# Second feed-forward projection of a hybrid decoder: seven block products for two of three token chunks

## The reference, cut to what matters

```python
x = _layer_norm(DN_ALPHA * x + mix, p['ln_mix_g'][i], p['ln_mix_b'][i])
hid = jnp.square(jax.nn.relu(x @ p['ffn_w1'][i]))                 # 1024 -> 4096
x = _layer_norm(DN_ALPHA * x + hid @ p['ffn_w2'][i], ...)          # 4096 -> 1024
```

## Time and profile before

| | us |
|---|---|
| median of 3 runs | 3169.58 (3167.16 to 3170.78) |
| profiled execution, its own time | 3167.34 |
| its span, first to last instruction | 3165.6 |
| PE busy | 3055.3 (97%) |
| weight loads (PEld) busy | 2841.0 (90%) |
| DVE busy | 1586.9 (50%) |
| POOL busy | 830.0 (26%) |
| ACT busy | 790.2 (25%) |

### The profile page before, as it was taken

One profiled execution on the slowest core, in us unless ns is written; L12 is line 12 of the kernel. 1 busy time (PEld: TensorE's weight loads), 2 busy tenths in 40 slices (PEclk: granted clock), 3 DMA queues, 4 the chain that ended last, 5 costly groups with the idle time before them and its releaser, 6 DMA issues.

```text
span 3165.6 us, 50120 instructions
## 1 busy us (share of the span) xinstructions
PE 3055.3 (97%) x20024; PEld 2841.0 (90%) x20024; DVE 1586.9 (50%) x2318; ACT 790.2 (25%) x1475; POOL 830.0 (26%) x523
## 2 busy tenths in 40 slices
PE   7998899999999999999989999998999999999997
PEld 7885789999999998999967878777999999999996
DVE  4877454333333354443358687878227333333335
ACT  4000442011111124111144444534106111111113
POOL 2232113333323232333201110113414232333330
PEclk9999999999999999999989999999999999999999
DMA  7555311111111113323255564747311111111111
GB/s 217 148 133 138 94 33 54 47 46 46 46 40 50 43 41 119 119 101 114 85 181 205 203 237 179 251 162 278 102 35 54 41 53 40 53 46 46 46 34 55
DMA packets 277968, 317.92 MB, mean 100 GB/s; under 512 B 25877, under 2 KB 217621, under 8 KB 276610
## 3 DMA queue, kind: packets, MB, share of 16 engines
q1 hardware_dynamic: 257577, 250.01, 25.6%
q10 hardware_dynamic: 12960, 40.04, 3.3%
q0 software_dynamic: 7296, 25.96, 2.4%
HBM read 224.63 MB, written 92.19 MB: 100 GB/s over the span
## 4 chain that ended last, share of the span: by engine, by line
PE 79%; DVE 10%; ACT 6%; issue 4%; DMA 1%; SPq 0%; POOL 0%; another core or an unknown queue 0%; DVEq 0%; ACTq 0%; POOLq 0%
PE ps L403 23%; PE ps L404 22%; PE ps L405 22%; PE ps L2068 2%; PE ps L1128 2%; PE ps L1171 1%; DVE CB L2489 1%; ACT X L486 1%; DVE CT L1565 1%; PE ps L1137 1%; PE ps L1138 1%; DVE RST L1729 1%; PE ps L1139 1%; PE ps L424 1%; DVE HT L1747 1%
## 5 line engine op out<-in xcount | busy, mean ns | idle before, releaser
L403 PE MATMUL ps<-AH,WH 128*128 128x352 f32 x3072 | 1000.4, 326 | 6.2 <-ACT SO L849 4.1
L404 PE MATMUL ps<-AL,WH 128*128 128x352 f32 x3072 | 986.2, 321 | 0.0
L405 PE MATMUL ps<-AH,WL 128*128 128x352 f32 x3072 | 985.7, 321 | 0.0
L388 POOL TENSOR_SCALAR WH<-RAW 128x1024 fp32r<-128x1024 f32 x200 | 236.0, 1180 | 1663.5 <-PEq L410 1467.7
L403 PEld LDWEIGHTS ps<-AH,WH 128*128 128x128 f32 x3072 | 577.6, 188 | 31.5 <-issue 22.6
L404 PEld LDWEIGHTS ps<-AL,WH 128*128 128x128 f32 x3072 | 578.7, 188 | 1.1 <-issue 0.2
L405 PEld LDWEIGHTS ps<-AH,WL 128*128 128x128 f32 x3072 | 577.5, 188 | 0.0
L390 POOL TENSOR_TENSOR WL<-RAW,WH 128x1024 fp32r<-128x1024 f32 x200 | 517.3, 2587 | 16.7
L403 PE MATMUL ps<-HH,WH 128*128 128x352 f32 x1536 | 498.4, 324 | 0.0
L404 PE MATMUL ps<-HL,WH 128*128 128x352 f32 x1536 | 492.2, 320 | 0.0
L405 PE MATMUL ps<-HH,WL 128*128 128x352 f32 x1536 | 491.9, 320 | 0.0
(11 more groups left out here) (317 smaller groups left out, 3392.3 us busy)
## 6 DMA issues: line engine op xcount, KB each, us to landing
RAW<-in_ffn_w SPq DMA_DIRECT2D x128, 512.0 KB, 3.6
CT<-in_state_mlstm_C SPq DMA_DIRECT2D x32, 1024.0 KB, 5.5
out_C_s<-CT SPq DMA_DIRECT2D x32, 1024.0 KB, 5.4
RAW<-in_ml_w_in SPq DMA_DIRECT2D x32, 512.0 KB, 3.9
RAW<-in_conv_w_pw SPq DMA_DIRECT2D x24, 512.0 KB, 7.9
STK<-u_scratch SPq DMA_DIRECT2D x64, 184.0 KB, 3.8
xc_scratch<-XC ACTq DMA_DIRECT2D x16, 528.0 KB, 2.7
so_scratch<-SO ACTq DMA_DIRECT2D x16, 528.0 KB, 3.7
```

Source lines behind the costliest of these rows:

```text
L388: pool.tensor_scalar(WH[:, k % 4], RAW[:, k % 2], 1.0, 0.0, ALU.mult, ALU.add).then_inc(w_hi, 1)
L403: pe.matmul(ps[:, bank, 0:CW], wh[:, k, cols], hi[:, k, cs], start=(k == 0), stop=False)
L404: pe.matmul(ps[:, bank, 0:CW], wh[:, k, cols], lo[:, k, cs], start=False, stop=False)
L405: mm = pe.matmul(ps[:, bank, 0:CW], wl[:, k, cols], hi[:, k, cs], start=False, stop=(k == nk - 1))
```

## The change

It touches the down phase of the blocks that are not the last, 7 in each of 2 layers. For chunks 0 and 1 the product of a 512x256 panel with the two chunks is split into halves in all three directions and done with seven products of half matrices instead of eight. The needed sums of weights and activations are formed before rounding. Chunk 2 stays a plain product. The last block is as before.

**PE.** For each panel g = 0..3 the products M1, M2, M5, P0, M6, M3, P1, M7 follow, and M4 of the panel before stands behind M1 (for g = 3 it closes the block). The M's have 6 matmuls each (`seven`), P0 and P1 are plain ones of 12:

```diff
+            for g in range(4):
+                m1(g)
+                if g:
+                    m4(g - 1)
+                m2(g)
+                m5(g)
+                plain(g, 0)
+                m6(g)
+                m3(g)
+                plain(g, 1)
+                m7(g)
+            m4(3)
```

M6, M7 and M4 accumulate onto M1 in one bank (6 or 7, by g), M3 onto M5 in another (1), M2 and the two plain ones have banks 0, 2 and 3. Since `X` takes the bank's content at every stage, each waits until DVE has added the one before:

```diff
+            def m1(g):
+                slot = weights(g, 0)
+                if g == 0:
+                    pe.wait_ge(F.relu, relu0 + (11 if first else 10))
+                    operand("corner")
+                elif g == 1:
+                    pe.wait_ge(F.relu, relu0 + 12)
+                added(g - 2, "M4")
+                seven(xbank(g), slot, 0, 0, *tile(0, 0), True, (F.mm, mm0 + 12, 2) if g == 0 else None)
+            def m4(g):
+                added(g, "M7")
+                operand("t")
+                seven(xbank(g), 2 * g % 4, 1, 1, *combined(1), False)
+            def m2(g):
+                added(g - 1, "M2")
+                seven(YB, 2 * g % 4, 1, 0, *tile(1, 0), True, (F.mm, mm0 + 12 + turn(g - 1, "M4") + 1, 2) if g else None)
+            def m5(g):
+                slot = weights(g, 1)
+                operand("t1")
+                added(g - 1, "M3")
+                seven(ZB, slot, 1, 1, *tile(0, 1), True)
+            def plain(g, h):
+                if h == 0:
+                    pe.wait_ge(F.relu, relu0 + 12)
+                operand("plain")
+                added(g - 1, ("P0", "P1")[h])
+                product(pe, PB[h], 2 * g % 4, 256, h, HH, HL, 4, ch[2]).then_inc(F.mm, 1)
```

**POOL.** A down panel is now two split panels with four sums of 128x256 between them, in place in `RAW`:

```diff
+                pool.tensor_scalar(WH[:, 2 * g % 4], raw, 1.0, 0.0, ALU.mult, ALU.add).then_inc(a_hi, 1)
+                pool.wait_ge(a_hi, na + 1)
+                pool.tensor_tensor(WL[:, 2 * g % 4], raw, WH[:, 2 * g % 4].bitcast(F32), ALU.subtract).then_inc(w_split, 1)
+                pool.wait_ge(w_split, n + 1)
+                pool.tensor_tensor(a22, a21, a22, ALU.add).then_inc(w_hi, 1)
...
+                pool.tensor_tensor(a21, a11, a21, ALU.subtract).then_inc(w_hi, 1)
...
+                pool.tensor_tensor(a11, a22, a11, ALU.subtract).then_inc(w_hi, 1)
...
+                pool.tensor_tensor(a12, a12, a11, ALU.subtract).then_inc(w_hi, 1)
...
+                pool.tensor_scalar(WH[:, (2 * g + 1) % 4], raw, 1.0, 0.0, ALU.mult, ALU.add).then_inc(a_hi, 1)
+                pool.wait_ge(a_hi, na + 2)
+                pool.tensor_tensor(WL[:, (2 * g + 1) % 4], raw, WH[:, (2 * g + 1) % 4].bitcast(F32), ALU.subtract).then_inc(w_split, 1)
```

**DVE and ACT.** The float32 squares go to `HR`, which lies where `HL` does, and the remainders are formed in place. When chunk 1 of a u is there (i = 3 and 9; in the first block 5 and 7), `combine` forms four sums, and one instruction each makes the remainders of two tiles (704 columns) or three (1056):

```diff
+                dve.wait_ge(F.sq, q)
+                dve.tensor_tensor(t3, b22, b12, ALU.subtract).then_inc(F.sq, 1)
+                dve.tensor_tensor(b12, b12, b11, ALU.subtract).then_inc(F.sq, 1)
...
+                dve.tensor_tensor(t2, b22, b12, ALU.subtract).then_inc(F.sq, 1)
...
+                dve.tensor_tensor(t4, b21, t2, ALU.subtract).then_inc(F.sq, 1)
...
+                low(HL[:, both, ch[0]], HR[:, both, ch[0]], HH[:, both, ch[0]])
...
+                low(HL[:, 2 * u, ch[1]], HR[:, 2 * u, ch[1]], HH[:, 2 * u, ch[1]])
...
+                low(TL[:, :, u], TR[:, :, u], TH[:, :, u])
+                low(HL[:, 2 * u + 1, ch[1]], HR[:, 2 * u + 1, ch[1]], HH[:, 2 * u + 1, ch[1]])
...
+                    if (c, h) == (2, 1):
+                        both = slice(2 * u, 2 * u + 2)
+                        dve.wait_ge(F.sq, sq0 + raw_order(first, i) + 1)
+                        dve.wait_ge(F.hh, hh0 + squared(first, i))
+                        low(HL[:, both, ch[2]], HR[:, both, ch[2]], HH[:, both, ch[2]])
```

ACT leaves out one square of six and rounds the combined operands instead, waiting for DVE's sums:

```diff
+            def combined_highs(u, hh):
+                act.wait_ge(F.sq, sq0 + combined_raw(first, u) + 2)
+                act.copy(HH[:, 2 * u, ch[1]], HR[:, 2 * u, ch[1]]).then_inc(F.hh, 1)
+                act.wait_ge(F.sq, sq0 + combined_raw(first, u) + 4)
+                act.copy(TH[:, :, u], TR[:, :, u]).then_inc(F.hh, 1)
```

More of the change, by code:

```diff
@@ L626, in ffn_loads @@
                     src, width = w2[bass.ds(b * 512, 512), (k - 4) * 256:(k - 3) * 256], 256
[L627 to L631, removed]
+                if last or k < 6:
+                    done = n + k - 1 if k or (isinstance(b, int) and b == 0) else n - 2
+                else:
+                    done = n + 2 * k - 6
@@ L672, in ffn_pe, with hidden_ready @@
                     ln_var_sum(pe, L, 2)
[L674 to L689, removed]
             if last:
+                def hidden_ready(c):
+                    n = 6 + 2 * c + 2
+                    pe.wait_ge(F.relu, relu0 + n)
+                    pe.wait_ge(F.hl, hl0 + n)
                 def by_chunk(c, u, between):
                     i = 4 * c + u
+                    k = 4 + u
                     if u == 0:
@@ L695, in by_chunk @@
                     if i >= 2:
[L696 to L707, removed]
@@ L709, in ffn_act @@
-        def ffn_act(act, l, b, first=False):
+                        pe.wait_ge(F.acc, acc0 + 2 * (i - 1))
+                    pe.wait_ge(w_split, panel_no(l, b, k) + 1)
+                    for h in range(2):
+                        release = None
+                        if h == 0 and (i == 0 or (c == 2 and u)):
+                            release = (F.mm, mm0 + 12 + 2 * i, 2 if i == 0 else 1)
+                        product(pe, bank_of(c, u, h), k % 4, 256, h, HH, HL, 4, ch[c], release).then_inc(F.mm, 1)
+                        if h == 0:
+                            between(c, u)
@@ new lines, in ffn_pe, with seven @@
+                ln_pe(pe, (ln_f0, ln_f1)[l], by_chunk, 4, F.acc, acc0)
+                free_panels(pe, F.mm, mm0 + 36, 1)
+                return
+            def seven(bank, slot, j, i, hi, lo, start, release=None):
+                for k in range(2):
+                    if k == 1 and release:
+                        free_panels(pe, *release)
+                    wh, wl = corner(WH[:, slot], j, i)[:, k], corner(WL[:, slot], j, i)[:, k]
+                    pe.matmul(ps[:, bank, 0:CW], wh, hi(k), start=(start and k == 0), stop=False, skip_group_check=True)
+                    pe.matmul(ps[:, bank, 0:CW], wh, lo(k), start=False, stop=False, skip_group_check=True)
+                    mm = pe.matmul(ps[:, bank, 0:CW], wl, hi(k), start=False, stop=(k == 1), skip_group_check=True)
+                mm.then_inc(F.mm, 1)
@@ new lines, in tile, with combined, weights, added @@
+            def tile(j, c):
+                return lambda k: HH[:, 2 * k + j, ch[c]], lambda k: HL[:, 2 * k + j, ch[c]]
+            def combined(m):
+                return lambda k: TH[:, m, k], lambda k: TL[:, m, k]
+            def weights(g, s):
+                pe.wait_ge(w_split, panel_no(l, b, 4 + 2 * g + s) + 1)
+                return (2 * g + s) % 4
+            def added(g, name):
+                if g >= 0:
+                    pe.wait_ge(F.acc, acc0 + turn(g, name) + 1)
+            def operand(item):
+                pe.wait_ge(F.hl, hl0 + ready(first, 1, item))
@@ new lines, in m6, with m3, m7 @@
+            def m6(g):
+                operand("t")
+                added(g, "M1")
+                seven(xbank(g), (2 * g + 1) % 4, 0, 0, *combined(0), False)
+            def m3(g):
+                operand("b22")
+                added(g, "M5")
+                seven(ZB, (2 * g + 1) % 4, 1, 0, *tile(1, 1), False)
+            def m7(g):
+                added(g, "M6")
+                seven(xbank(g), (2 * g + 1) % 4, 0, 1, *combined(2), False)
+            for g in range(4):
[9 more added lines that the diff above has]
+                m7(g)
@@ L729, in ffn_dve @@
             L = (ln_m0, ln_m1)[l]
[L730 to L737 removed]
+            mm0, acc0, relu0 = F.nmm + 48 * b, F.nacc + 36 * b, F.nrelu + 12 * b
@@ L2349, in _ @@
             ffn_act(act, 0, 0, True)
-            with act.Fori(1, FB) as b:
+            with act.Fori(1, FB - 1) as b:
                 ffn_act(act, 0, b)
+            ffn_act(act, 0, FB - 1, last=True)
             ln_act(act, ln_f0, R_FFNG, R_FFNB, 4)
@@ L2415, in _ @@
             ffn_act(act, 1, 0, True)
-            with act.Fori(1, FB) as b:
+            with act.Fori(1, FB - 1) as b:
                 ffn_act(act, 1, b)
+            ffn_act(act, 1, FB - 1, last=True)
             ln_act(act, ln_f1, R_FFNG + 1, R_FFNB + 1, 4, split=False)
```

252 lines of the change are left out of this document (192 added, 60 removed).

## The result

The changed kernel is **slower by 0.7%**: 3192.21 us (median of 4 runs, 3190.25 to 3193.25) against 3169.03 us (median of 4), a ratio of 1.0068 with a 95% interval of 1.0056 to 1.0080. The profiled execution took 3192.95 us with a span of 3191.2, so 25.6 us of span more than the execution profiled before.

What follows compares the result with a forecast made beforehand. PE was taken to bound the kernel, at 0.159 us a matmul. Terms -53.4 + 32.2 + 14.0 + 2.1 + 13.5 + 4.0 = +12.4 us took the median from 3169.58 to 3182 us, range 3150 to 3206.

Steps and rivals of the forecast that it cites:

- likeliest case: Whole kernel: all six terms together add 12.4 us, median 3182 us, own range 3169 to 3194; chance 0.60.
- Term 1: Down phases on PE: 336 matmuls removed at 0.159 us each, -53.4 us.
- Term 2: Start of down phase: P0(0) waits 2.3 us for DVE's last remainders, held by POOL, in 14 blocks: +32.2 us.
- Rival A: Start of down phase: P0(0)'s wait on the remainders does not occur; 3150 us, faster; chance 0.13.
- Term 3: End of down phase: closing M4(3) waits for the add of M7(3), 1.0 us in 14 blocks: +14.0 us.
- Term 4: Down phase: the 42 other M4s, with M1 of the next panel between, wait 0.05 us each: +2.1 us.
- Term 5: Two first blocks: M1(0) waits for ACT's late Relu of product 10, 7.0 us each, less 0.2: +13.5 us.
- Term 6: Behind the two first blocks' stops: granted clock falls to the 1.2 GHz level, 2.0 us each: +4.0 us.
- At nothing, POOL: Down phase: POOL's second split costs nothing; pair takes 10.4 us of 10.7 us room, 0.3 spare.
- Rival C: Down phase: POOL bounds from turn to turn, M5 waits 0.75 us in two turns of 14 blocks; 3203; chance 0.12.
- Rival B: Down phases: the saving comes nearly whole, only the closing M4s wait; 3130 us; chance 0.05.
- Rival D: Inner blocks: clock falls after each 2.3 us wait too, 12 more times up to 1.7 us; 3202; chance 0.10.

Runs made afterwards that it cites:

- Experiment 8: Changed kernel with POOL's panel-1 remainder held behind DVE's last, M7(3) ahead of P1(3), and each layer's first block as before the change: 3133.97 us, ratio 0.9885.
- Experiments 1: Changed kernel plus one wait: POOL begins the remainder of panel 1's first split only after DVE's last hidden-phase remainder: 3153.28 us, ratio 0.9940.
- experiment 2: Changed kernel plus a wait for DVE's last hidden-phase remainder before POOL's first instruction (the rounding) of panel 1's split: 3159.17 us, ratio 0.9968.
- Experiment 3: Changed kernel with the last turn's order M3, M7, P1, M4 on PE and DVE, so P1 stands before the closing M4: 3181.51 us, ratio 1.0033.
- Experiment 6: Changed kernel with ACT's three alpha multiplications two hidden products earlier in each layer's first block: 3195.64 us, ratio 1.0076.
- experiment 5: Changed kernel with a fifth 256-column sum, overwritten at once, in each of POOL's pairs of splits: 3193.48 us, ratio 1.0077.
- experiments 7: Changed kernel with POOL's panel-1 remainder behind DVE's last, M7(3) before P1(3), and ACT's alpha multiplications earlier in first blocks: 3140.50 us, ratio 0.9906.
- 4: Changed kernel with the first block of each layer as before the change, blocks 1 to 6 as changed: 3174.72 us, ratio 1.0010.

## Why the prediction was right

The forecast's case came in, with its sum 10 us too low: 3192.2 against 3182, inside the likeliest case's own range of 3169 to 3194. Step by step:

- **Term 1, right.** 336 matmuls fewer, 3.82 us of PE a block. Experiment 8 shows that they are worth nearly that where no wait takes their place.
- **Term 2, right.** P0(0) waits on the remainders in 14 blocks, since DVE's instruction is issued 0.41 us behind POOL's. Experiments 1 and 2 show the cause: the order alone removes the wait. The size was 2.17 us in an inner block instead of 2.3 (listed 1.90; beyond the usual 0.159 from start to start PE lost 2.07, and the following matmul is 0.10 late). The remainder ended at +4.87 instead of +4.97. **Rival A** is out with it.
- **Term 3, right.** 0.97 us a block, listed 0.70: M4 starts 1.03 us after M7's last matmul instead of 0.16, and the matmul behind it is 0.10 late. Experiment 3 gives 1.1 from the periods and 11 us in all.
- **Term 4** had 0.05 for each of 42 others. None is listed, and in block 1 an M4 starts 0.16 us behind the matmul ahead of it (616.39, 616.55). The inner block does lose 0.4 us beside the two waits (3.82 less 2.17, 0.97 and the 0.31 that it gained), but spread over many matmuls: the 24 from 616.23 on take 3.93 us instead of 3.82. Why is open.
- **Term 5, right in sum by luck, for the wrong reason.** I had 13.5 us (7.0 less 0.2, twice, is 13.6). Against plain first blocks the two cost 14.8, where terms 5, 6 and the first blocks' shares of the others made 16.8 (13.5 + 4.0 + 2 x (2.3 + 1.0 + 0.15 - 3.82)). The step that failed is "they now take turns": DVE issued the first three sums of its second set, to 487.32, before POOL began at 487.35, and only the fourth was held (1.41 us). The fourth ended at 488.76; the prediction's 489.6 is 492.6 here, where the feed-forward starts 3.0 us later. So M1(0) waited 2.4 us, not 7. But POOL's pair then lay later, on top of the squares and the last remainders: 3.94 us for two squares, and P0(0) waited 4.8 us where I had put 2.3. Experiment 6 shows that ACT's multiplications were not the cause.
- **Term 6** had 2.0 us behind each of these two stops. The clock does fall there, and for longer than I took from the earlier trace rows: the granted clock of 0.77, 0.50 and 0.88 in the three windows of 4 us from 500 to 512 us is 6.8 us at half rate, and in layer 1 0.82, 0.50, 0.50 and 0.90 from 2452 to 2468 us is 10.2, against 4.8 ((3 x 0.50 + 3 x 0.30) x 2) in the earlier trace rows. PE stood still in part of it, so what it cost is not known apart; it is part of the 14.8 us above.
- **At nothing, POOL, right.** There is no wait on `WL` in inner blocks. In block 1 POOL's second remainder ends at 618.06 and M5 starts at 618.52, on time; by the 0.13 us from panel to PE of experiment 2 the spare was 0.3 us, and experiment 5 gives 0.2. So the predicted 0.3 was right, but from two errors of one size. The pair took 10.63 us and not 10.4: its terms as written make 10.51, and a gap of 0.27 us stands where I had 0.08. And its room from POOL's start was 11.0 us (607.42 to 618.52, less 0.13), not 10.7. **Rival C** is out, though 0.6 us more of POOL a pair brings 0.8 us a block of it.
- **Rival B** is out; its 3130 us is about what experiment 8 gives, where the waits and the first blocks' new order are gone.
- **Rival D came in by half**, and is why the sum was low. I had the clock fall behind the first blocks' stop alone. It fell in seven of twelve inner blocks, at 1.57 us each (I had up to 1.7): 11.0 us. Without them the measured time would be 3181. The step of the prediction that failed is term 6: it has the clock fall behind two stops only and puts twelve inner stops of 2.3 us at nothing, though rows showed a fall behind one of 4.1 us.

The account of the 25.6 us of span between the two profiled executions, read from the marks: the twelve inner periods add up to 6.7 us more (without the clock 12 x (91.25 - 91.56) = -3.7, the seven falls +11.0, and the shorter last ones of each layer). The two first blocks are 15.2 us longer than before, read from DVE's second remainder of the feed-forward's input to the first mark: 107.4 and 108.3 us instead of 100.3 and 100.2. The other 3.7 us are in places that the change does not touch: the feed-forward of layer 0 begins 3.0 us later (444.31 instead of 441.36 for that remainder), the stretch between the two feed-forwards is 1.3 us shorter, and from the last mark to the end it is 2.0 us longer, nearly all of it behind the last instruction of ACT, where the output is written.

The 3.0 us come from the token mixer of layer 0, in which the clock stood at half rate elsewhere. The window from 300 to 320 us shows it, in the kernel before:

```profile
300.00:320.00 20.00, 15.91 (x254) 7.38 (x250) 6.96 (x5) 5.55 (x6) 0.00 (x0) 1.00 0.07 13
```

and in the changed kernel, with 42 matmuls fewer and a clock of 0.83:

```profile
300.00:320.00 20.00, 15.98 (x212) 6.77 (x208) 4.35 (x4) 5.19 (x5) 0.00 (x0) 0.83 0.04 7
```

A DVE add of this stretch that starts at 338.07 us before starts at 341.43 in the changed kernel, at 338.64 in experiment 2 and at 342.49 in experiment 8. So these 3 to 4 us are in some kernels' executions and not in others', with the same code up to there. That they are chance was not tested by repeats.

## What to carry to other kernels

A saving on the bounding engine is worth its count of instructions only where no operand arrives later: here 24 matmuls, 3.82 us a block, were eaten by one 2 us wait, one 1 us wait and falls of the clock, and all three went from the inner blocks with one semaphore wait put in and one product moved (experiments 7 and 8). When the order of products changes, ask whose result is now due earlier: chunk 2's was needed 7.6 us into the down phase and now 2.9 us into it. Where two engines hold each other up, as DVE and POOL do here, write down which instruction is issued first at the one moment that matters, and put the one that the critical engine waits for in front: a semaphore wait on the other engine made a loss of 0.7% a gain of 0.6%. And a wait is put down to what ended last: check in the code that the waiting instruction has a wait for it, as with M5(1) in experiment 2.

## What the runs showed of the hardware

- **The clock falls behind a stop of about 2 us, but not always.** The granted clock went to its 1.2 GHz level in 7 of 12 inner blocks of the changed kernel, about 3.5 us each, after a stop of PE that is alike in all twelve (listed 1.9 us). Experiments 3, 4 and 6, with the same stop, have 8, 6 and 8. Without the stop (the kernel before and experiments 1, 2, 7 and 8) it never fell in an inner block. But the stop alone does not decide: experiment 5 has it in twelve blocks and no fall. What else decides is open. The period differs there (91.9 to 92.4 us throughout), but no run varied that alone.
- **A pair of POOL's has a gap I had not counted.** Between the last sum and the second rounding stand two semaphore waits and an increment, where two sums have one wait between them. The changed kernel's POOL timeline:

```profile
613.50 0.75 POOL L680 TENSOR_TENSOR RAW<-RAW 128x256 f32<-128x256 f32 x1
614.52 1.06 POOL L685 TENSOR_SCALAR WH<-RAW 128x1024 fp32r<-128x1024 f32 x1 [0.27 <-POOL RAW L680]
```

  The gap is 0.27 us where the sums stand 0.08 apart. Which of the three instructions costs it was not tested; with a sum put in behind the waits (experiment 5) there is 0.16 us ahead of that sum and none behind it. The 256-column sum itself took 0.74 to 0.75 us, as read between the lines of the earlier trace rows.
- **A tie between DVE and POOL.** In the rows shown above the instruction issued first ran on and the other waited. In the first block three sums of DVE, issued ahead, ran at 0.52 us each. The fourth was issued at 487.35, in the same hundredth as POOL's rounding: POOL's ended at 488.40 and DVE's at 488.76, so POOL went first. It is one instance and no more.
